# Expert 0's context rows picked by a one-hot product between top-k rounds, and its context products put ahead of the gather

## The reference, cut to what matters

```python
x = x + g1 * (o @ w_out)                                  # x1 below
h2 = rmsnorm(x, norm2_g) * (1 + sc2) + sh2                # other sc2, sh2 for context tokens
aff = softmax(h2 @ w_router)                              # 16 experts
gate, idx = top_k(aff.T, cap)                             # per expert: 64 latent tokens, 16 context tokens
xs = h2[idx]
out = (silu(xs @ w_gate) * (xs @ w_up)) @ w_down * gate   # w_gate, w_up: 2048x1024 for each expert
x = x + g2 * scatter_add(out, idx);  y = rmsnorm(x, final_norm_g)
```

## Time and profile before

| | |
|---|---|
| three runs, median (lowest to highest) | 2103.51 us (2102.74 to 2106.03) |
| profiled execution, span | 2099.3 us |
| top-k's first max starts | 1060.24 us |
| lists turned (L1223) from | 1071.91 us |
| gather issued | 1075.69 us |
| first gate/up product | 1083.38 us |
| first down product of expert 0 | 1127.88 us |
| one expert in the steady part | 61.80 us |

### The profile page before, as it was taken

How to read it: one execution, slowest core, us unless ns; L and a number is a source line. 1 busy time by engine, 2 the same in 40 slices (tenths; PEclk the granted TensorE clock), 3 DMA queues, 4 the chain that set the end, 5 groups by cost and what they waited for, 6 DMA issues and landing times. The chain is left out here.

```text
span 2099.3 us, 37670 instructions
## 1 busy us (share of the span) xinstructions
PE 2027.9 (97%) x15045; PEld 1128.7 (54%) x15045; DVE 1139.3 (54%) x2673; ACT 478.1 (23%) x846; POOL 165.3 (8%) x236
## 2 busy tenths in 40 slices
PE   6999999999999999999979999999999999999995
PEld 3578878888878887888842333333333333333331
DVE  4369988997558877777255243343233333223314
ACT  4232222222257776222210000000000000000003
POOL 1020010111000001112110000000000000000001
PEclk9999999999999999999989999999999999999998
DMA  9956667563120006665489999999999999999997
GB/s 389 409 188 219 213 231 257 202 221 112 69 103 1 2 1 236 227 201 187 158 308 378 406 413 417 416 416 421 424 416 416 417 416 415 429 416 416 417 395 318
DMA packets 71924, 614.03 MB, mean 292 GB/s; under 512 B 8432, under 2 KB 10104, under 8 KB 29104
## 3 DMA queue, kind: packets, MB, share of 16 engines
q1 hardware_dynamic: 47392, 514.36, 59.3%
q0 software_dynamic: 18672, 84.89, 13.3%
q10 hardware_dynamic: 5776, 13.63, 1.9%
HBM read 583.28 MB, written 29.60 MB: 292 GB/s over the span
## 5 line engine op out<-in xcount | busy, mean ns | idle before, releaser
L1261 PE MATMUL ps<-arena 128*32 128x512 f32 x6144 | 662.6, 592 | 0.6 <-DVE arena L2315 0.6
L1261 PEld LDWEIGHTS ps<-arena 128*32 128x32 f32 x6144 | 199.4, 110 | 458.6 <-issue 457.7
L1288 PE MATMUL ps<-arena 128*32 128x512 f32 x3072 | 332.8, 592 | 2.6 <-DVE arena L2326 1.8
L702 PE MATMUL ps<-B_w_hi,B_x_hi 128*128 128x512 f32 x720 | 286.7, 398 | 6.0 <-DVE B_x_lo L2098 3.3
L704 PE MATMUL ps<-B_w_lo,B_x_hi 128*128 128x512 f32 x720 | 281.5, 391 | 0.0
L703 PE MATMUL ps<-B_w_hi,B_x_lo 128*128 128x512 f32 x720 | 281.3, 391 | 0.0
L1288 PEld LDWEIGHTS ps<-arena 128*32 128x32 f32 x3072 | 99.6, 110 | 232.9 <-issue 228.6
L2347 DVE COPY arena<-arena 128x16 f32 x1200 | 156.6, 182 | 98.6 <-issue 98.6
L2323 DVE TENSOR_TENSOR arena<-ps,arena 64x256 f32<-64x256 f32 x96 | 39.9, 416 | 297.9 <-ACT arena L1618 297.3
L1618 ACT ACTIVATE arena<-ps 64x512 f32<-64x512 f32 x48 | 28.5, 594 | 609.0 <-PE ps L1261 609.0
L702 PEld LDWEIGHTS ps<-B_w_hi,B_x_hi 128*128 128x128 f32 x720 | 135.5, 188 | 45.6 <-issue 12.6
(11 more groups left out here) (286 smaller groups left out, 2027.4 us busy)
## 6 DMA issues: line engine op xcount, KB each, us to landing
arena<-in_w_expert SPq DMA_DIRECT2D x192, 2048.0 KB, 12.8
arena<-in_w_in_b SPq DMA_DIRECT2D x36, 1024.0 KB, 5.0
arena<-in_w_mod_q SPq DMA_DIRECT2D x32, 1024.0 KB, 19.2
arena<-in_w_mod POOLq DMA_DIRECT2D x32, 1024.0 KB, 5.7
arena<-in_w_mod POOLq DMA_DIRECT2D x32, 512.0 KB, 4.3
arena<-in_w_out_b SPq DMA_DIRECT2D x16, 1024.0 KB, 6.4
arena<-in_w_mod POOLq DMA_DIRECT2D x64, 256.0 KB, 3.3
arena<-in_x_sample SPq DMA_DIRECT2D x8, 1024.0 KB, 10.2
```

Source lines behind the costliest of these rows:

```text
L702: eng.matmul(out, x_hi, w_hi, start=start, stop=False)
L1261: mm = pe.matmul(bank(g)[32 * q:32 * q + 32, :], e_rows, w[q], start=start, stop=stop, skip_group_check=True)
L1288: mm = pe.matmul(bank(b)[32 * q:32 * q + 32, :], hT[g][:, f, :], w_four[q], start=f == 0, stop=f == 7, skip_group_check=True)
```

## The change

While top-k still runs, TensorE builds the context rows of expert 0 by a product. After two rounds VectorE converts the context lists (`idxf[:, 0:CX]`); TensorE broadcasts expert 0's 16 context indices to all partitions (bank 5); after round 3's max_index VectorE compares them with each partition's token number and multiplies by the norm factor (`picked`, a scaled one-hot matrix of 128x16). TensorE multiplies the 16 chunks of the context tile of x1 with it; 12 chunks come from `x1_d` by a new load on SP's queue (`ctx_rows`, 768 KB, ahead of units 2 to 5) and 4 from the x1 in SBUF. ScalarE turns each chunk into `xC` (16 activations with scale and bias). TensorE then runs the context products of pairs 0 and 1, the latent lists, those of pairs 2 and 3, the places, and those of pairs 4 and 5 (`CTX_AHEAD` = 6), all ahead of its wait for the gathered rows. The gather fetches 64 rows without factors; a compare with the row number and a sum on VectorE pick the 64 factors (`r_picked`), ScalarE makes a diagonal `spread` of them, and the transposes of the gathered rows become products with it. ScalarE's three loads of `fgB` and `G2` no longer stand behind the gather. The 22 unread products become 14 ahead of the broadcast and 6 behind the context lists. The copies of the factors into `x1_d` go (one on VectorE, five stores on GpSimd's queue), and the zeroing of `xC` moves ahead of the seam.

The diff, cut to its core:

```diff
@@ SP @@
                 after_out(sp, 2 * c + 1)
+                if c == 15:
+                    sp.wait_ge(early_stored, 96)
+                    sp.dma_start(ctx_rows, x1_d[LAT:TOK, 0:3 * NB]).then_inc(ctx_in, 16)
                 for u in us:
                     unit_e(0, u)
@@ TensorE @@
             low, high, ctx = (ident[0:4 * NE, NE * g:NE * (g + 1)] for g in (0, 2, 1))
+            for _ in range(14):
+                pe.matmul(bank(0)[:, 0:P], ident[:, :], ident[:, :], start=True, stop=True, skip_group_check=True)
             pe.wait_ge(route_ready, 3)
+            pe.matmul(bank(5)[:, 0:CX], ctx[:, 0:1].broadcast_to([4 * NE, P]), idxf[:, 0:CX], start=True, stop=True,
+                      skip_group_check=True).then_inc(route_turned, 1)
...
+            for _ in range(6):
+                pe.matmul(bank(0)[:, 0:P], ident[:, :], ident[:, :], start=True, stop=True, skip_group_check=True)
+            pe.wait_ge(ctx_in, 16)
             pe.wait_ge(route_ready, 4)
-            pe.wait_ge(flip_ready, 1)
...
-            for _ in range(22):
-                pe.matmul(bank(0)[:, 0:P], ident[:, :], ident[:, :], start=True, stop=True, skip_group_check=True)
...
+            left, right = by_pairs(ctx_rows), by_pairs(x1[:, TL, 3 * NB:D])
+            for k in range(KC):
+                cols = left[:, k // 2, k % 2, :] if k < 12 else right[:, (k - 12) // 2, k % 2, :]
+                mm = pe.matmul(bank(0)[:, CX * k:CX * (k + 1)], cols, picked, start=True, stop=True, skip_group_check=True)
+            mm.then_inc(t1_done, 1)
...
-                    pe.wait_ge(xs_scaled, g + 1)
+                    pe.wait_ge(gathered, 16)
+                    pe.wait_ge(spread_ready, 1)
                     for k in range(k0, k0 + n):
-                        mm = pe.transpose(bank(b)[:, CAP * (k - k0):CAP * (k - k0 + 1)], xsP[0:CAP, P * k:P * (k + 1)],
-                                          ident[0:CAP, 0:CAP])
+                        mm = pe.matmul(bank(b)[:, CL * (k - k0):CL * (k - k0 + 1)], xs_cols[:, k // 2, k % 2, :],
+                                       spread[0:CL, :], start=True, stop=True, skip_group_check=True)
...
+            def context_ahead(i):
+
+                landed(0, i)
+                pe.wait_ge(xC_ready, 2 * i + 2)
+                context_pair(i)
...
-                    latent_pair(e, i, (0, 1))
-                    context_pair(i)
+                    last = latent_pair(e, i, (0, 1))
+                    if not first or i >= CTX_AHEAD:
+                        last = context_pair(i)
+                    last.then_inc(xused, 2)
...
-            pe.wait_ge(route_ready, 5)
+            context_ahead(0)
+            context_ahead(1)
+            latent_lists()
+            context_ahead(2)
+            context_ahead(3)
+            column_places()
+            for i in range(4, CTX_AHEAD):
+                context_ahead(i)
+            pe.wait_ge(route_ready, 7)
             gathered_transposes((0, 1))
@@ ScalarE @@
-            act.wait_ge(gathered, 16)
-            for k0, n, _ in FIRST:
-                cols = slice(P * k0, P * (k0 + n))
-                act.activation(xsP[0:CAP, cols]..., by_pairs(xs[0:CAP, cols]), ACT.Copy, scale=xs[0:CAP, D:D + 1])
-            act.wait_ge(cols_ready, 2)
+            act.wait_ge(t1_done, 1)
+            act.wait_ge(xC_zero, 1)
+            for k in range(KC):
+                act.activation(xC[:, k, 0:CX], bank(0)[:, CX * k:CX * (k + 1)], ACT.Identity, bias=modT[:, 3, 1, k:k + 1],
+                               scale=A2[:, 1, k:k + 1]).then_inc(xC_ready, 1)
+            act.wait_ge(cols_ready, 4)
+            act.activation(spread[0:CL, :], ident[0:CL, 0:CL], ACT.Copy, scale=r_picked[:, 0:1]).then_inc(spread_ready, 1)
@@ GpSimd @@
-            for t in range(NT):
-                pool.dma_start(x1_d[P * t:P * (t + 1), D:D + ROW_PAD], rstdP[:, t, :]).then_inc(r_stored, 16)
...
+            pool.iota(tok_row, [[1, LAT]], base=0, channel_multiplier=0, allow_small_or_imprecise_dtypes=True)\
+                .then_inc(flip_ready, 1)
...
-            pool.indirect_dma_start(xs[0:CAP, :], None, x1_d[:, :],
-                                    bass.IndirectOffsetOnAxis(ap=idxC[:, 0:1], axis=0)).then_inc(gathered, 16)
+            pool.indirect_dma_start(xs[0:CL, :], None, x1_d[:, :],
+                                    bass.IndirectOffsetOnAxis(ap=idxC[0:CL, 0:1], axis=0)).then_inc(gathered, 16)
@@ VectorE @@
                 link(dve.max_index(idx[:, top], vals[:, top], row))
+                if r == CX // 8 - 1:
+                    dve.tensor_copy(idxf[:, 0:CX], idx[:, 0:CX]).then_inc(route_ready, 1)
+                if r == CX // 8:
+                    dve.wait_ge(route_turned, 3)
+                    dve.wait_ge(const_ready, 2)
+                    dve.tensor_scalar(picked, bank(5)[:, 0:CX], tok_id[:, 0:1], rstd2[:, TL:TL + 1], ALU.is_equal, ALU.mult)\
+                        .then_inc(route_ready, 1)
                 if r < CL // 8 - 1:
                     link(dve.match_replace(affT, vals[:, top], row, -1.0))
...
+            link(dve.scalar_tensor_tensor(out=tok_row, in0=tok_row, scalar=row_of[0:CL, 0:1], in1=bank(6)[0:CL, 0:LAT],
+                                          op0=ALU.is_equal, op1=ALU.mult))
+            dve.tensor_reduce(r_picked[:, :], tok_row, AX, ALU.add).then_inc(cols_ready, 1)
```

More of the change, by code:

```diff
@@ L413, in build @@
         oT_hi, oT_lo = [parts_D["oT_hi"][i] for i in HI_AT], parts_D["oT_lo"]
-        xs = at(H0, D + ROW_PAD)
-        xsP = at(W0 + 4096, D)
+        xs = at(H0, D)
+        tok_row = at(W0 + 4608, LAT)[0:CL, :]
+        spread = at(W0 + 4096, CL)
+        picked = at(W0 + 4096 + CL, CX)
         xstage = at(H0 + 2064, KC, CAP)
@@ L427, in build @@
         xrow_out = at(H0 + 4880, D)
+        ctx_rows = at(H0 + 4880, 3 * NB)
         assert 4880 + D <= 6928 and L0 - SLOT == H0 + 8192
@@ L591, in build @@
         gathered = sem("gathered")
[L592 removed]
+        spread_ready = sem("spread_ready")
+        ctx_in = sem("ctx_in")
+        xC_ready = sem("xC_ready")
         t1_done = sem("t1_done")
@@ L1225, in _ @@
[L1225 to L1229, removed]
-            pe.wait_ge(route_ready, 4)
-            pe.wait_ge(flip_ready, 1)
-            pe.matmul(bank(4)[0:CL, 0:2 * NE], flip, slots[:, 1].rearrange("p n e -> p (n e)"), start=True, stop=True,
-                      skip_group_check=True).then_inc(route_turned, 1)
@@ L1234, in _ @@
-            for _ in range(22):
-                pe.matmul(bank(0)[:, 0:P], ident[:, :], ident[:, :], start=True, stop=True, skip_group_check=True)
-            pe.wait_ge(cols_ready, 2)
-            pe.wait_ge(cols_ready, 3)
-            pe.matmul(bank(7)[0:NE, 3 * P:3 * P + CAP], off_of[:, :], ident[0:CAP, 0:CAP], start=True, stop=True,
-                      skip_group_check=True).then_inc(route_turned, 1)
+                pe.matmul(bank(7)[CL:CAP, 4 * P - 2 * NE + NE * n:4 * P - 2 * NE + NE * (n + 1)], what[:, 0:CX], ctx, start=True,
+                          stop=True, skip_group_check=True)
@@ new lines, in _, with latent_lists @@
+            mm.then_inc(t1_done, 1)
+            def latent_lists():
+                pe.wait_ge(route_ready, 5)
+                for n, what in ((0, idxf), (1, vals)):
+                    for half, rows in ((1, high), (0, low)):
+                        mm = pe.matmul(bank(3)[0:CL, NE * (2 * half + n):NE * (2 * half + n + 1)], what, rows, start=True,
+                                       stop=True, skip_group_check=True)
+                mm.then_inc(route_turned, 1)
+                pe.wait_ge(route_ready, 6)
+                pe.wait_ge(flip_ready, 1)
+                pe.matmul(bank(4)[0:CL, 0:2 * NE], flip, slots[:, 1].rearrange("p n e -> p (n e)"), start=True, stop=True,
+                          skip_group_check=True).then_inc(route_turned, 1)
@@ L1242, in gathered_transposes, with column_places @@
+            def column_places():
+                pe.wait_ge(cols_ready, 2)
+                pe.wait_ge(cols_ready, 3)
+                pe.matmul(bank(7)[0:NE, 3 * P:3 * P + CAP], off_of[:, :], ident[0:CAP, 0:CAP], start=True, stop=True,
+                          skip_group_check=True).then_inc(route_turned, 1)
+            xs_cols = by_pairs(xs[0:CL, 0:D])
             def gathered_transposes(only):
```

74 lines of the change are left out of this document (37 added, 37 removed).

## The result

The changed kernel is slower: ratio 1.0026 to the kernel before, 95% interval 1.0020 to 1.0033, median 2108.18 us in 16 runs against 2102.16 us in 16 runs of the kernel before. The profiled execution spans 2105.3 us, 6.0 more than before. The prediction had +3.2 us, 2106.7 us, with a range from 2101.0 to 2111.5.

A forecast was written before the change was run, and what follows sets the result against it. The prediction took VectorE's chain from the fourth group of rows to bound expert 0, TensorE everything behind the seam. -3.7 + 4.9 + 2.4 - 0.4 = +3.2 us on 2103.5 gave 2106.7 us, range 2101.0 to 2111.5.

The forecast's parts named there:

- the 10.3 us: Expert 0: six context pairs, 12 rounds at full clock, leave TensorE's stretch behind the start of gate/up work.
- The fast rival: Expert 0: TensorE is the bound, all 10.3 us count and no hole opens; -8.9 us, 2094.6 us; chance 0.12.
- Fewer products before the last group: Expert 0, ahead of the fourth group of gathered rows: two context pairs fewer bring the down products forward; -3.7 us.
- L: Start of TensorE's gate/up work on expert 0: 1083.38 before the change, forecast 1088.2.
- Two context pairs go from this, 4 rounds, 3.43 us: From gate/up start to VectorE's five multiplications: 12.74 us before, shorter by two context pairs; multiplications start 9.0 us in.
- A later L: Seam: expert 0's gate/up work starts later, lists at 1078.4 plus 9.85 us; +4.9 us.
- some waits between them: From latent lists to gate/up start: TensorE's four context pairs, flip, places and waits take 8.8 us; whole stretch 9.85 us.
- The clock behind the hole: Expert 0's down products begin at half clock after TensorE idles 8.4 us; +2.4 us, between 1.5 and 3.6.
- The last expert's wait: Last expert: TensorE's 0.73 us wait for a weight unit may go or stay; -0.4 us.
- Hidden things: Beside other work: the `ctx_rows` load, zeroing of `xC`, dropped stores and weight units were expected to stay hidden.
- the slow one: Seam: half clock from the one-hot products to the lists, start of gate/up 7.5 us later; +5.8 us, 2109.3 us; chance 0.26.
- The clock holds: Seam: TensorE's clock does not fall, gate/up starts only 1.4 us later; -0.3 us, 2103.2 us; chance 0.24.

The follow-up runs named there:

- e1_ctx2: Changed kernel with only context pairs 0 and 1 ahead of the gathered rows, 32 unread products in place of pairs 2 to 5; 1.0024, 2106.38 us.
- e2_inter: Changed kernel with VectorE's five multiplications of x1 by the norm factors put between the groups of gathered rows; 0.9989 to the kernel before, 2099.53 us.
- e7_before_inter: Kernel before the change with VectorE's five multiplications put between the groups of gathered rows; 0.9992, 2099.82 us.
- e11_turn_ctx2: e6_turn with only context pairs 0 and 1 ahead, 32 unread products in place of pairs 2 to 5; 1.0000 to the kernel before, 2101.78 us.
- e10_turn_few: e6_turn with 5 instead of 14 unread products ahead of the broadcast, the other 6 kept; 0.9958 to the kernel before, 2093.11 us.
- e6_turn: e2_inter with latent lists behind one context pair, GpSimd's copies behind the places, gathered rows scaled on ScalarE and transposed again; 0.9974 to the kernel before, 2095.15 us.
- e3_port: Changed kernel with GpSimd's five copies of x1's last quarter waiting until VectorE has picked the factors; 1.0026 to the kernel before, 2108.13 us.
- e12_warm: Changed kernel with 32 unread products in the hole before expert 0's down products; 1.0018 to the kernel before, 2105.64 us.
- e4_lists: Changed kernel with the latent lists behind one context pair instead of two; 1.0026 to the kernel before, 2106.79 us.
- e9_least: e6_turn with 2 instead of 14 unread products ahead of the broadcast and 2 instead of 6 behind the context lists; 0.9969, 2096.16 us.
- e8_few: e2_inter with lists behind one context pair, GpSimd's copies behind the places, 5 instead of 14 unread products ahead of the broadcast; 0.9968, 2094.72 us.

## Why the prediction was right, and where its terms were off

The sign, the place and the mechanism were right. Nothing of the 10.3 us reached the end because VectorE's chain hangs on the fourth group of rows, behind two pairs only; e1_ctx2, e2_inter, e7_before_inter and e11_turn_ctx2 show this from four sides. The fast rival (TensorE binds, 2094.6 us) fell with e1_ctx2, and e10_turn_few came to a like time, 2093.1 us, by removing the bound and more.

The size was not right: 6.0 us for 3.2, with every term of the sum off and the errors partly cancelling. Two things make it look better than it was. The 2106.7 us stand on a median of three runs, 2103.5, where 16 runs gave 2102.16; on that base the forecast would be 2105.4, 2.8 us too low. And the prediction gave a slowdown of over 0.2% only 0.34, and 0.54 to no change within 0.2%; the ratio is 1.0026. The terms, with what each measured:

- **Fewer products before the last group, -3.7.** Measured -2.0: from L the multiplications start 10.7 us later, not 9.0. The two pairs did become 3.4 us shorter and the context operations' 0.25 us came too; the step that failed is "Two context pairs go from this, 4 rounds, 3.43 us", which left the products of groups 2 and 3 at the price of the transposes. They have two records for each chunk, the transposes one, and took 1.62 us for six chunks (e6_turn: 0.59), in all some 1.65 us more ahead of the multiplications.
- **A later L, +4.9.** Measured +6.7 (1090.06 against 1083.38). The lists were turned at 1078.07, forecast 1078.4, but by errors that cancel: the one-hot products ran at full clock, against the forecast (3.84 us, and 1.00 in the stretch), the stall in round 3 was 2.4 and not 1.5 us, for the 14 unread products took 3.84 us and not 3.0, and the clock fell under the context pairs (5.34 us, where the later pairs took 3.64). That the lists came on time is luck. Behind them to L were 12.0 us, not 9.85. The step put the places in "some waits between them"; TensorE waited 1.93 us for VectorE's L2352, which ran beside GpSimd's copies (e3_port), and the products of groups 0 and 1 took 1.6 us together.
- **The clock behind the hole, +2.4.** Measured +1.33, below the forecast's lower end of 1.5; e12_warm took it away. The clock came back after some 2.7 us of work (twice 1.33, an estimate; the stretch from 1132.5 to 1135 shows 0.50). Behind the same hole it cost 2.10 us in e3_port and 1.64 in e4_lists, so the term was nearer than the one profile says.
- **The last expert's wait, -0.4.** Measured +0.4, and given back at the very end, so 0 in the sum.
- **Hidden things.** `ctx_rows` landed in 6.2 us and nobody waited for it; the weight units did not hold expert 0.

The nearest rival in time was the slow one (2109.3 us), but its mechanism, half clock from the one-hot products on, did not occur in the changed kernel's profile. It did in e9_least, with 2 unread products instead of 14. *The clock holds* is wrong too: 0.50 at 1074 to 1077.

The rule of the Trainium skill that the prediction weighed (TensorE: Matmul & The Clock Gate, What's actually happening), taken as the busy time of the profile, fits the one-hot products of this one profile: TensorE was busy, and the clock was 1.00. Other profiles speak against that reading. In e2_inter, with the same 14 and 6 unread products ahead and no wait, the clock fell while the one-hot products ran; they took 4.43 us, and from 1071 to 1072 TensorE was busy throughout at a granted clock of 0.72, from 1071 to 1074 at 0.57:

```profile
1071.00:1074.00 3.00, 2.20 (x15) 2.00 (x19) 2.79 (x11) 1.08 (x5) 0.00 (x0) 0.57 0.66 276
```

In e9_least TensorE was busy for 3.35 of 3.40 us from 1065 to 1068.4 at 0.50. In every profile with context pairs ahead the first of them ran at least partly at 0.50. So the prediction's "I expect the clock to fall during the one-hot products and to return during the first context pairs" is what e2_inter shows; in the changed kernel's profile the clock fell only behind them. Why it falls under a busy TensorE stays open.

## What to carry to other kernels

Before counting products that leave a stretch, look for the engine that ends the stretch's only hole, and for the point where its chain is tied to the other engine: only work ahead of that point counts, here 4 rounds of 12. A hole of 1.8 us is a warning that the next saving on that engine will be paid out as idle time, and idle time of 8 us costs its clock as well. Then look for work of the binding chain that fits into that engine's own idle gaps: moving five multiplications gave 7.8 us where 10 us of moved products had given a loss. And give the old kernel the same help before crediting the new one: with the multiplications moved in both, the two can't be told apart (e7_before_inter, e2_inter).

## What the runs showed that was not expected

- **Two engines on one port.** L2352, a VectorE operation on 80x16 values, took 2.34 us beside GpSimd's copies of 128x512, and 0.17 us when they were held behind it (e3_port). In the kernel before it took 0.54 us and ended as the copies began. The last of L2350's three took 0.63 instead of 0.17 us. The compare (L2356), with a PSUM operand, took 0.73 us with the last copy beside most of it and 0.74 us without. The Trainium skill (SBUF — State Buffer, SBUF: two separate sides) says that VectorE and GpSimd share a pair of ports as an exclusive lock, taken among others by a VectorE operation with two SBUF inputs against a GpSimd operation that reads SBUF; whichever starts first keeps it for its whole instruction. The slowed lines have two such inputs, the compare one. The trace agrees in kind, 2.34 against 0.17 us, but L2352 stood through four copies of 0.61 us each and not through one. L2350's slow one ended at 1082.29, 0.07 us ahead of the first copy's recorded start; GpSimd's recorded times are rough, so which operation held it is not shown.
- **A diagonal product is no cheap transpose** in fp32: two records and 0.27 us a chunk against one record and 0.10 us (e6_turn).
- **Unread products can be worth their time, up to a point.** Of 14, 9 could go (e8_few, e10_turn_few: the seam 1.0 and 3.0 us shorter, the latter with 1.4 us of it from a faster clock further on); with 12 and 4 gone the one-hot products went from 3.84 to 5.70 us (e9_least). These are single profiles; of the eleven with 5 or 14 and 6 unread products ten show 3.84 us and one 4.43 (e2_inter).
